# Convolution taps of the VectorE moved between attention blocks in a one-core hybrid decoder step

## The chip, the cores and the metric

The program runs on one core of a Trainium2 chip (eight cores in two dies). The metric is device time in microseconds of one execution. Engines are called by their names in the profile: PE is TensorE, DVE VectorE, ACT ScalarE, POOL GpSimd, SP SyncE.

## The reference, cut to what matters

One layer of a decoder for a prompt of 1024 tokens and 8 sample sequences of 4 tokens (1056 columns in all). One input projection feeds three branches: a gated linear recurrence, stick-breaking attention and a convolution module. The change touches the order of work in the last two:

```python
def _sb_block(q, k, v, bias, q_pos, k_pos):
    z = jnp.einsum('bhqd,bhkd->bhqk', q, k) * (SB_HEAD_DIM ** -0.5) + bias[None, :, None, None]
    mask = k_pos[None, :] < q_pos[:, None]
    log_rest = jnp.where(mask, jax.nn.log_sigmoid(-z), 0.0)
    tail = lax.cumsum(log_rest, axis=3, reverse=True) - log_rest
    A = jnp.where(mask, jnp.exp(jax.nn.log_sigmoid(z) + tail), 0.0)
    return jnp.einsum('bhqk,bhkd->bhqd', A, v)

c = _causal_dwconv(u_full, W['conv_w'][l], W['conv_b'][l])   # 31 taps per channel, before LayerNorm, swish, w_pc
```

The attention is causal in query blocks of 128 tokens: block q of the prompt looks at 128 (q + 1) keys, so block 0 is 128 keys wide and block 7 is 1024 wide.

## The kernel before, in words

Everything is kept transposed, 128 channels on the partitions and 1056 tokens along them. After an opening (RMSNorm, five projection units) come four groups, p = 0 to 3, of 128 channels each; the first three run in a loop, the last is written out. A group holds one pair of attention heads, 128 convolution channels and one recurrence head. After the groups come the branch projections, the output projection and the feed-forward part, which the diff leaves alone.

All five engines run their own program, and the order on each is written out by hand; they meet through semaphores, whose helper `wait` is a method of `Signal`. On DVE a chain semaphore (`Chain`) keeps dependent instructions apart.

**Projection units as filler.** The projection of the group after (and the gates) is cut into units. One unit is 128 output channels: 8 k-steps of 9 matmuls (hi and lo halves of the weights and of the activations, three column thirds of 352), recorded at L367. `fill(n)` on PE issues n such k-steps between attention steps, in the pattern `A_FILL = (2, 2, 3, 1)`, so one attention block holds exactly one unit. All units accumulate in the same PSUM banks 0 to 2. So the first k-step of a unit waits until ACT has copied the unit before out of PSUM (`stage_unit`, the ACTIVATE at L895). That copy stands at the head of the next block in ACT's order. When a unit is done, POOL splits the weights that come two units later (CAST L344, then TENSOR_TENSOR L346), and SP loads the next ones (L337) once the split is over.

**One attention block q**, two heads e = 0, 1:
- PE: scores, first 512 keys (L604); transposes of head 0's weights of block q-1 (L615); fill(2); from block 4 on the scores of the other keys (L604); fill(2); transposes of head 1 of block q-1 (L615); fill(3); product with the values of block q-1 (L626); fill(1), which ends the unit.
- ACT: stage_unit of the last unit (L895), copies of the scores with bias (L943), softplus of each head as Exp and Ln (L950, L952), copies of the transposed weights (L966), final exponential of each head (L958, `weights_of`). Head 1's `weights_of` is the last of the block, and the stage_unit of the next block stands behind it.
- DVE: for each head `scores_read`, the mask on the diagonal (L1272) and the clip (L1275); then for each head `tail_sum`, that is a max (L1282), a reversed scan (L1284) and a subtract (L1285), which releases `weights_of` on ACT.

Small sample work is mixed in: in block 1 PE makes the sample scores (L635) once SP's cache loads have landed; in block 2 DVE masks, clips and scans the sample row (L1293, L1294, L1301, L1303, L1304); in block 3 ACT makes its exponential (L988), for which the PE waits before it transposes it (L643); in block 4 come the sample values (L653).

**The convolution on DVE.** One tap is a multiply-add over 1024 prompt columns (L1256) and a small one over the 32 sample columns (L1257); the first tap is L1259 and L1260. Each tap first waits for the tap before it. `tap()` issues the next one and does nothing once all 31 are out. Before the change it stands at four places in each block: between mask and clip of head 0 and of head 1 (in `scores_read`), before the tail sum of head 0, and between the two tail sums. That gives taps 0 to 27 in blocks 0 to 6 and the last three in block 7, the last before the tail sum of head 0. The last tap releases SP's stores of the convolution (L432 to L435), which in SP's order stand behind a gate store that waits for ACT's copy at the head of the step after block 7.

```python
                    dg = z[:, q * P:n]
                    ch.mark(dve.tensor_tensor(dg, dg, neg, ALU.add))
                    tap()
                    ch.wait()
                    dve.tensor_scalar(l, z, ZMAX, None, ALU.min).then_inc(e_ready.sem, 1)
```

Of the kernel before, what the change touches and what calls it, by code (L numbers as in the profile page):

```python
# [40 lines left out]
QB = TP // P  # L41
Z_CHUNKS = [q if q < 4 else 4 + 2 * (q - 4) for q in range(QB + 1)]
A_FILL = (2, 2, 3, 1)
H_FILL = (4, 4, 3, 3, 3, 3, 3, 3, 3, 3, 4, 4)
GPG = 5
NGATE = 3 * KD
# [55 lines left out]
def build(nc, dr):  # L102
    ctx = ExitStack()
    with ctx:
# [84 lines left out]
        def par(name, j=0, n=1):  # L189
            a = PK[name][0] + j  # L190
            return pk[:, a:a + n]
# [367 lines left out]
        def _(pe):  # L559
# [48 lines left out]
            def turn_a(p, i):  # L608
                a_ready.wait(pe, p, i + 1)
                if i:  # L610
                    at_ready.wait(pe, p, i)
                if i == 8:
                    os_read.wait(pe, p, 1)
                for kb in range(i // 2 + 1):
                    mm = pe.transpose(banks(5, 1024)[:, kb * P:(kb + 1) * P],  # L615
                                      zb[2 * (i // 2 % 2) + i % 2][:, kb * P:(kb + 1) * P], ident)
                mm.then_inc(t_done.sem, 1)

            def values(p, q):

                at_ready.wait(pe, p, 2 * q + 2)
                if q:
                    o_read.wait(pe, p, q)
                for kb in range(q + 1):
                    for e in range(2):
                        mm = pe.matmul(ps[DH * e:DH * e + DH, 7, (q % 4) * P:(q % 4 + 1) * P],  # L626
                                       vtok[:, kb, DH * e:DH * e + DH], atv[e][:, kb * P:(kb + 1) * P],
                                       start=(kb == 0), stop=(kb == q))
                mm.then_inc(av_done.sem, 1)
# [17 lines left out]
            def sample_values(p):  # L647
                ats_ready.wait(pe, p, 1)
                pe.matmul(ps[:, 6, 256:320], vtok[0:SM, 8, :], ats[0:SM, 2, :], start=True, stop=False,
                          skip_group_check=True)  # L650
                for b in range(NSEQ):
                    for g in range(NPG):
                        mm = pe.matmul(ps[:, 6, 256 + 8 * b:264 + 8 * b], vsv[:, b, g, :], ats[:, g, 8 * b:8 * b + 8],  # L653
                                       start=False, stop=(b == NSEQ - 1 and g == NPG - 1), skip_group_check=True)
                mm.then_inc(os_done.sem, 1)
# [7 lines left out]
            def turn9(src, b0):  # L663

                for c in range(CH):
                    pe.transpose(banks(b0, 1024)[:, c * P:(c + 1) * P], src[:, c * P:(c + 1) * P], ident)
                return pe.transpose(ps[0:SM, 7, 0:P], src[:, TP:T], ident)

            def level_product(p, idx, left, right, b0, sample):
                for c in range(CH):  # L670
                    mm = pe.matmul(banks(b0, 1024)[:, c * P:(c + 1) * P], left[:, c * P:(c + 1) * P],  # L671
                                   right[:, c * P:(c + 1) * P], start=True, stop=True)
                if sample:
                    mm = pe.matmul(ps[0:SM, 7, 0:SM], left[:, TP:T], right[:, TP:T], start=True, stop=True)
                mm.then_inc(lev_done.sem, 1)

            def group(p, more):
                at_k = [0]

                def fill(n):  # L680

                    for _ in range(n):
                        jj, k = divmod(at_k[0], KD)
                        if jj < units(more):
                            unit_part(PRE + jj, p, (k,))
                            at_k[0] += 1
# [3 lines left out]
                for q in range(QB + 1):  # L690
# [4 lines left out]
                    if q:  # L695
                        turn_a(p, 2 * q - 2)
                    fill(A_FILL[0])
                    if 4 <= q < QB:
# [5 lines left out]
                    if q == 4:  # L704
                        sample_values(p)
                    fill(A_FILL[1])
                    if q:
                        turn_a(p, 2 * q - 1)
                    fill(A_FILL[2])
                    if q:  # L710
                        values(p, q - 1)
                    fill(A_FILL[3])

# [3 lines left out]
                turn9(iT, 5).then_inc(ia_turned.sem, 1)  # L717
                fill(H_FILL[0])
                qk_ready.wait(pe, p, 1)
                va_staged.wait(pe, p, 1)  # L720
                level_product(p, 0, kk, qA, 3, True)
                fill(H_FILL[1])
                for j in range(NL):
# [4 lines left out]
                    if j < 5:  # L728
                        fill(H_FILL[2 + j])
                fill(H_FILL[7])  # L730
                kd_ready.wait(pe, p, 1)
                att_read.wait(pe, p, NL + 1)
                turn9(kd, 3).then_inc(kd_turned.sem, 1)
                fill(H_FILL[8])
                kdt_staged.wait(pe, p, 1)
# [8 lines left out]
                mm.then_inc(um_done.sem, 1)  # L744
                fill(H_FILL[9])
                s_ready.wait(pe, p, 1)
# [445 lines left out]
        def _(dve):  # L1192
# [23 lines left out]
            def group(p, more):  # L1216
# [32 lines left out]
                def tap(last=False):  # L1249
                    w = taps[0]  # L1250
                    if w >= CW:
                        return
                    taps[0] += 1
                    if w:
                        ch.wait()
                        ch.mark(dve.scalar_tensor_tensor(ca, up[:, w:w + TP], cwp[:, w:w + 1], ca, ALU.mult, ALU.add))  # L1256
                        ins = dve.scalar_tensor_tensor(cs, us[:, :, w:w + TS], cwp[:, w:w + 1], cs, ALU.mult, ALU.add)  # L1257
                    else:
                        ch.mark(dve.tensor_scalar(ca, up[:, 0:TP], cwp[:, 0:1], cwp[:, CW:CW + 1], ALU.mult, ALU.add))  # L1259
                        ins = dve.tensor_scalar(cs, us[:, :, 0:TS], cwp[:, 0:1], cwp[:, CW:CW + 1], ALU.mult, ALU.add)  # L1260
                    if w == CW - 1:
                        ins.then_inc(conv_done.sem, 1)
                    else:
                        ch.mark(ins)

                def scores_read(q, e):

                    i, n = 2 * q + e, P * (q + 1)
                    z, l = zb[2 * (q % 2) + e][:, 0:n], lb[e][:, 0:n]
                    z_read.wait(dve, p, 2 * Z_CHUNKS[q + 1] - 1 + e)  # L1270
                    dg = z[:, q * P:n]
                    ch.mark(dve.tensor_tensor(dg, dg, neg, ALU.add))  # L1272
                    tap()
                    ch.wait()
                    dve.tensor_scalar(l, z, ZMAX, None, ALU.min).then_inc(e_ready.sem, 1)  # L1275

                def tail_sum(q, e):

                    i, n = 2 * q + e, P * (q + 1)
                    z, l = zb[2 * (q % 2) + e][:, 0:n], lb[e][:, 0:n]  # L1280
                    ln_ready.wait(dve, p, i + 1)
                    ch.link(dve.tensor_tensor(l, z, l, ALU.max))  # L1282
                    r = l[:, ::-1]
                    ch.link(dve.tensor_tensor_scan(r, r, r, 0.0, ALU.add, ALU.max))  # L1284
                    dve.tensor_tensor(z, z, l, ALU.subtract).then_inc(arg_ready.sem, 1)  # L1285

                zs, ls = A(A_ZS, SBK, slice(0, 64)), A(A_LS, SBK, slice(0, 64))
                for q in range(QB):
                    scores_read(q, 0)
                    scores_read(q, 1)  # L1290
                    if q == 2:
                        zs_read.wait(dve, p, 1)
                        ch.link(dve.tensor_tensor(zs[:, PAST:], zs[:, PAST:], par("neg_new", 0, SM)[0:64, :], ALU.add))  # L1293
                        dve.tensor_scalar(ls, zs, ZMAX, None, ALU.min).then_inc(es_ready.sem, 1)  # L1294
                    tap()
                    tail_sum(q, 0)
                    tap()
                    tail_sum(q, 1)
                    if q == 2:
                        lns_ready.wait(dve, p, 1)  # L1300
                        ch.link(dve.tensor_tensor(ls, zs, ls, ALU.max))  # L1301
                        r = ls[:, ::-1]
                        ch.link(dve.tensor_tensor_scan(r, r, r, 0.0, ALU.add, ALU.max))  # L1303
                        dve.tensor_tensor(zs, zs, ls, ALU.subtract).then_inc(args_ready.sem, 1)  # L1304
                while taps[0] < CW:
                    tap()

# [105 lines left out]
            with dve.Fori(0, NH - 1) as p:  # L1413
                group(p, True)
            group(NH - 1, False)


# [231 lines left out]
```

## Time and profile before

| | |
|---|---|
| median of 3 runs | 2382.62 us (2382.07 to 2383.61) |
| the profiled execution's own time | 2382.67 us |
| its span, first to last instruction | 2380.9 us |
| mean granted TensorE clock | 0.941 |
| PE busy | 2086.1 us (88%) |
| DVE busy | 1101.2 us (46%) |
| ACT busy | 610.0 us (26%) |
| POOL busy | 591.3 us (25%) |

Busy times are sums over an engine's instructions. PE is busy for 88% of the span, but that is an average: the groups fill about the first half, and there PE has gaps. In a view of stretches each row is from A to B of the span (here from the end of one stage_unit copy to the next), its length, the busy us of PE, PEld, DVE, ACT and POOL with their counts, the granted TensorE clock (PEclk), the DMA share and GB/s. An idle time in brackets behind a row says how long the engine had waited just before that instruction, and what ended the wait.

### The profile page before, as it was taken

Reading aid. Unit: us, or ns where it says so; the run is one execution under the profiler, and the core shown is the slowest. Engines: PE = TensorE matmul, PEld = TensorE weight load, DVE = VectorE, ACT = ScalarE, POOL = GpSimd, SP = SyncE. Lnnn points to the kernel's source line nnn. Section 1 sums busy time; section 2 is a strip of 40 time slices with the busy share of each in tenths; the row PEclk is TensorE's granted clock in tenths of the full one; section 3 lists DMA queues with packets and bytes.
Section 4 is the critical chain, followed back from the end, with each engine's and each line's share of the span. In section 5 each row is a group of like instructions: output and inputs, shape, how many; then the busy total and the mean of one; then the engine's idle time right before and its main releaser. Section 6 shows DMA issues by size and latency. Waiting matters only on the chain.

```text
span 2380.9 us, 32200 instructions
## 1 busy us (share of the span) xinstructions
PE 2086.1 (88%) x12832; PEld 1984.5 (83%) x12832; DVE 1101.2 (46%) x1169; ACT 610.0 (26%) x792; POOL 591.3 (25%) x392
## 2 busy tenths in 40 slices
PE   7898789977999779997787989879999999999994
PEld 5887688867888678886787889759999999999993
DVE  3267465664547655566543653362223222222235
ACT  3234322344134342334312522130101001001011
POOL 1211211121111112111212232242333332323332
PEclk9999899988999889998898999889999999999997
DMA  4221203111031111310225331311111111111121
GB/s 138 61 82 31 66 19 117 49 36 57 19 120 46 36 57 37 119 36 27 75 83 184 109 122 47 123 69 41 40 57 31 48 52 32 53 40 40 57 104 77
DMA packets 203987, 156.89 MB, mean 66 GB/s; under 512 B 15730, under 2 KB 188402, under 8 KB 203890
## 3 DMA queue, kind: packets, MB, share of 16 engines
q1 hardware_dynamic: 201698, 146.89, 19.7%
q10 hardware_dynamic: 2192, 8.65, 0.9%
q8 instruction: 68, 1.11, 0.2%
q14 instruction: 29, 0.24, 0.0%
HBM read 120.16 MB, written 35.35 MB: 65 GB/s over the span
## 4 chain that ended last, share of the span: by engine, by line
PE 68%; DVE 18%; ACT 6%; issue 5%; DMA 1%; SPq 1%; POOL 0%; POOLq 0%; DVEq 0%; ACTq 0%
PE psum L367 59%; DVE arena L1284 3%; PE psum L671 2%; DVE arena L1256 2%; DVE arena L1282 1%; DVE arena L1257 1%; PE psum L604 1%; PE psum L572 1%; DVE hid L1523 1%; DVE arena L1272 1%; PE psum L653 1%; DVE ug L1285 1%; DVE mix L1508 1%; PE psum L626 1%; DVE arena L1285 1%
## 5 line engine op out<-in xcount | busy, mean ns | idle before, releaser
L367 PE MATMUL psum<-h_hi,w_hi 128*128 128x352 f32 x2400 | 557.2, 342 | 157.3 <-ACT gate_logits L895 61.2
L367 PEld LDWEIGHTS psum<-h_hi,w_hi 128*128 128x128 f32 x2400 | 416.8, 197 | 184.6 <-issue 163.4
L367 PE MATMUL psum<-h_lo,w_hi 128*128 128x352 f32 x2400 | 533.9, 332 | 0.0
L367 PE MATMUL psum<-h_hi,w_lo 128*128 128x352 f32 x2400 | 530.7, 330 | 0.0
L367 PEld LDWEIGHTS psum<-h_lo,w_hi 128*128 128x128 f32 x2400 | 425.5, 196 | 0.0
L367 PEld LDWEIGHTS psum<-h_hi,w_lo 128*128 128x128 f32 x2400 | 424.4, 194 | 0.0
L344 POOL CAST w_hi<-w_raw 128x1024 fp32r<-128x1024 f32 x60 | 71.8, 1197 | 967.5 <-PE psum L367 948.6
L357 POOL CAST w_hi<-w_raw 128x512 fp32r<-128x512 f32 (+1 forms) x128 | 96.5, 754 | 736.6 <-PE psum L367 642.0
L359 POOL TENSOR_TENSOR w_lo<-w_raw,w_hi 128x512 fp32r<-128x512 f32 (+1 forms) x128 | 227.8, 1780 | 10.3
L1173 ACT ACTIVATE hid<-psum 128x1056 f32<-128x1056 f32 x32 | 33.7, 1054 | 583.1 <-PE psum L367 583.1
L367 PE MATMUL psum<-hid_hi,w_hi 128*128 128x352 f32 x768 | 166.4, 325 | 10.8 <-DVE hid_lo L1525 10.8
L1532 DVE TENSOR_TENSOR ff_sum<-ff_sum,psum 128x1056 f32<-128x1056 f32 x56 | 70.2, 1254 | 227.4 <-PE psum L367 227.4
L1523 DVE TENSOR_TENSOR hid<-hid 128x1056 f32<-128x1056 f32 x32 | 54.4, 1699 | 254.2 <-ACT hid L1173 254.2
L367 PE MATMUL psum<-hid_lo,w_hi 128*128 128x352 f32 x768 | 166.7, 325 | 0.0
L367 PE MATMUL psum<-hid_hi,w_lo 128*128 128x352 f32 x768 | 165.7, 324 | 0.0
L346 POOL TENSOR_TENSOR w_lo<-w_raw,w_hi 128x1024 fp32r<-128x1024 f32 x60 | 156.9, 2614 | 4.8
L1256 DVE SCALAR_TENSOR_TENSOR arena<-arena,conv_w_now 128x1024 f32<-128x1024 f32 x120 | 153.7, 1281 | 2.1
L367 PEld LDWEIGHTS psum<-hid_hi,w_hi 128*128 128x128 f32 x768 | 130.9, 188 | 13.0 <-DVE hid_lo L1525 13.0
L367 PEld LDWEIGHTS psum<-hid_lo,w_hi 128*128 128x128 f32 x768 | 131.1, 188 | 0.0
L367 PEld LDWEIGHTS psum<-hid_hi,w_lo 128*128 128x128 f32 x768 | 130.6, 188 | 0.0
L1284 DVE TENSOR_TENSOR_SCAN arena<-arena 128x128 f32<-128x128 f32 (+7 forms) x64 | 109.5, 1711 | 2.2
L1272 DVE TENSOR_TENSOR arena<-arena,params 128x128 f32<-128x128 f32 x48 | 22.1, 461 | 163.3 <-ACT arena L943 163.3
(237 smaller groups left out, 2417.9 us busy)
## 6 DMA issues: line engine op xcount, KB each, us to landing
w_raw<-in_w_in SPq DMA_DIRECT2D x60, 512.0 KB, 4.1
w_raw<-in_w_ff SPq DMA_DIRECT2D x32, 512.0 KB, 4.0
w_raw<-in_w_ff SPq DMA_DIRECT2D x64, 256.0 KB, 2.7
g_d<-gate_logits SPq DMA_DIRECT2D x24, 528.0 KB, 3.1
gates<-g_d SPq DMA_DIRECT2D x24, 528.0 KB, 3.6
arena<-in_xT SPq DMA_DIRECT2D x8, 528.0 KB, 7.3
x_again<-in_xT SPq DMA_DIRECT2D x1, 4224.0 KB, 13.8
x_d<-x_again ACTq DMA_DIRECT2D x8, 528.0 KB, 2.7
```

Source lines behind the costliest of these rows:

```text
L344: pool.tensor_copy(wh[:, s, :, :], raw[:, s, :, :]).then_inc(w_hi_set, 1)
L346: pool.tensor_tensor(wl[:, s, :, :], raw[:, s, :, :], wh[:, s, :, :].bitcast(F32), ALU.subtract).then_inc(w_split, 1)
L357: pool.tensor_copy(wh[:, slot, 0:kt, :], raw[:, slot, 0:kt, :]).then_inc(w_hi_set, 1)
L359: pool.tensor_tensor(wl[:, slot, 0:kt, :], raw[:, slot, 0:kt, :], wh[:, slot, 0:kt, :].bitcast(F32), ALU.subtract).then_inc(w_split, 1)
L367: mm = pe.matmul(ps[:, b0 + g, 0:GW], w[:, slot, k, :], x[:, k, g * GW:(g + 1) * GW], start=(k == 0 and w is wh and x is xh), stop=(k == k ...
L671: mm = pe.matmul(banks(b0, 1024)[:, c * P:(c + 1) * P], left[:, c * P:(c + 1) * P], right[:, c * P:(c + 1) * P], start=True, stop=True)
L1256: ch.mark(dve.scalar_tensor_tensor(ca, up[:, w:w + TP], cwp[:, w:w + 1], ca, ALU.mult, ALU.add))
L1272: ch.mark(dve.tensor_tensor(dg, dg, neg, ALU.add))
L1284: ch.link(dve.tensor_tensor_scan(r, r, r, 0.0, ALU.add, ALU.max))
L1285: dve.tensor_tensor(z, z, l, ALU.subtract).then_inc(arg_ready.sem, 1)
L1523: dve.tensor_tensor(h, h, h, ALU.mult).then_inc(hid_sq, 1)
L1532: dve.tensor_tensor(v3(acc[:, j, :]), v3(acc[:, j, :]), psg(3 * (j % 2)), ALU.add)\
```

## The change

A new tuple `EARLY` says how many extra taps stand at the end of each block. In blocks 0 to 3 all four old places stay, and 4, 4, 2 and 1 taps are added behind the tail sum of head 1 (in block 2 behind the sample's scan too). In blocks 4 to 7 only the place before the tail sum of head 0 keeps its tap. So blocks 0 to 3 hold 8, 8, 6 and 5 taps and blocks 4 to 7 one each, 31 in all as before, and the last stands where it stood.

```diff
+EARLY = (4, 4, 2, 1, 0, 0, 0, 0)
...
                     dg = z[:, q * P:n]
                     ch.mark(dve.tensor_tensor(dg, dg, neg, ALU.add))
-                    tap()
+                    if q < 4:
+                        tap()
                     ch.wait()
...
                     tap()
                     tail_sum(q, 0)
-                    tap()
+                    if q < 4:
+                        tap()
                     tail_sum(q, 1)
...
                         dve.tensor_tensor(zs, zs, ls, ALU.subtract).then_inc(args_ready.sem, 1)
+                    for _ in range(EARLY[q]):
+                        tap()
                 while taps[0] < CW:
                     tap()
```

## Rows read from the trace of the kernel before

**Rows 1.** Who waited for whom, PE: total us, times, longest us

```profile
PE psum L367 <- ACT gate_logits L895: 61.2, 11, 7.3
PE psum L367 <- ACT gA L895: 32.8, 4, 8.3
...
PE psum L643 <- ACT arena L988: 10.3, 4, 3.0
```

**Rows 2.** Group 1, blocks 2, 4 to 7: length, busy PE, PEld, DVE, ACT, POOL, PEclk

```profile
425.05:441.15 16.10, 14.52 (x95) 13.16 (x93) 15.28 (x21) 6.53 (x16) 5.39 (x4) 1.00 0.20 67
...
460.47:483.04 22.57, 22.57 (x143) 21.09 (x144) 13.29 (x18) 8.68 (x16) 3.44 (x3) 0.85 0.14 48
483.04:507.10 24.06, 16.95 (x120) 15.15 (x120) 17.20 (x18) 9.45 (x15) 6.81 (x4) 0.96 0.08 22
507.10:534.65 27.55, 19.38 (x125) 17.76 (x125) 18.40 (x18) 10.32 (x15) 4.74 (x2) 0.81 0.20 58
534.65:562.23 27.58, 18.88 (x123) 17.37 (x123) 18.11 (x16) 11.38 (x15) 6.29 (x2) 0.81 0.00 1
```

**Rows 3.** DVE in order of time, group 1, block 6 and end of block 7

```profile
514.37 1.28 DVE L1256 SCALAR_TENSOR_TENSOR arena<-arena,conv_w_now 128x1024 f32<-128x1024 f32 x1
...
515.86 0.63 DVE L1275 TENSOR_SCALAR arena<-arena 128x896 f32<-128x896 f32 x1
...
521.22 2.02 DVE L1284 TENSOR_TENSOR_SCAN arena<-arena 128x896 f32<-128x896 f32 x1
...
524.29 1.28 DVE L1256 SCALAR_TENSOR_TENSOR arena<-arena,conv_w_now 128x1024 f32<-128x1024 f32 x1
525.49 1.03 DVE L1257 SCALAR_TENSOR_TENSOR arena<-arena,conv_w_now 128x32 f32<-128x32 f32 x1
...
527.55 4.04 DVE L1284 TENSOR_TENSOR_SCAN arena<-arena 128x896 f32<-128x896 f32 x1
531.63 1.09 DVE L1285 TENSOR_TENSOR arena<-arena 128x896 f32<-128x896 f32 x1
...
549.24 2.29 DVE L1284 TENSOR_TENSOR_SCAN arena<-arena 128x1024 f32<-128x1024 f32 x1
...
553.97 3.01 DVE L1284 TENSOR_TENSOR_SCAN arena<-arena 128x1024 f32<-128x1024 f32 x1
557.01 3.18 DVE L1285 TENSOR_TENSOR ug<-ug,arena 128x1024 f32<-128x1024 f32 x1
```

**Rows 4.** POOL in order of time, groups 0 (block 1) and 1 (blocks 0, 6)

```profile
136.88 1.04 POOL L344 CAST w_hi<-w_raw 128x1024 fp32r<-128x1024 f32 x1 [20.17 <-PE psum L367]
...
403.10 2.37 POOL L346 TENSOR_TENSOR w_lo<-w_raw,w_hi 128x1024 fp32r<-128x1024 f32 x1
...
524.89 1.58 POOL L344 CAST w_hi<-w_raw 128x1024 fp32r<-128x1024 f32 x1 [22.22 <-PE psum L367]
526.55 3.16 POOL L346 TENSOR_TENSOR w_lo<-w_raw,w_hi 128x1024 fp32r<-128x1024 f32 x1
```

**Rows 5.** PE in order of time, three matmuls a row, start of block 6

```profile
507.23 1.22 PE L367 MATMUL psum<-h_hi,w_hi 128*128 128x352 f32 x3 [7.25 <-ACT gate_logits L895]
508.25 1.08 PE L367 MATMUL psum<-h_lo,w_hi 128*128 128x352 f32 x3
...
513.91 0.64 PE L367 MATMUL psum<-h_lo,w_hi 128*128 128x352 f32 x3
```

**Rows 6.** DVE in order of time, group 0, blocks 1 and 2

```profile
118.53 0.29 DVE L1272 TENSOR_TENSOR arena<-arena,params 128x128 f32<-128x128 f32 x1 [1.68 <-ACT arena L943]
...
131.47 0.43 DVE L1282 TENSOR_TENSOR arena<-ug,arena 128x256 f32<-128x256 f32 x1 [4.58 <-ACT arena L952]
...
138.31 2.24 DVE L1272 TENSOR_TENSOR arena<-arena,params 128x128 f32<-128x128 f32 x1 [5.22 <-ACT arena L943]
...
152.33 2.60 DVE L1301 TENSOR_TENSOR arena<-arena 64x288 f32<-64x288 f32 x1
```

**Rows 7.** One line of the program: min/median/max ns of all 120

```profile
L1256 DVE SCALAR_TENSOR_TENSOR arena<-arena,conv_w_now x120: 1269/1282/1287, 107.8 to 1126.8; 128x1024 f32<-128x1024 f32 x120
```

## The prediction

> **What bounds it.** The list of PE's waits comes first: the longest, 61.2 us in 11 waits, is PE's filler waiting for ACT's copy of a gate unit, and 32.8 us in 4 more for the copy of gA [rows 1]. That copy is ACT's first work in a block, but in ACT's order it stands behind the last exponential of the block before, which DVE's last subtract releases. So PE waits for DVE's chain. The view of stretches says where: blocks 6 and 7 last 27.55 and 27.58 us with PE busy for 19.38 and 18.88, block 5 24.06 with 16.95, while block 4 is 22.57 us long and PE is busy for all of it [rows 2]. DVE is busy for 17 to 18 us in blocks 5 to 7, in one unbroken run from the mask to the last subtract. There every DVE microsecond is one on the path; in block 4 none is. The wait repeats once a block, four groups long. Block 2 is another kind: DVE is busy 15.28 of its 16.10 us [rows 2], and at its end hangs the sample chain (DVE, ACT's exponential, PE's transpose), for which PE waits up to 3.0 us in each of four groups [rows 1].
>
> **What leaves the wide blocks.** Eleven taps of a group move: three each from blocks 4, 5 and 6, two from block 7. No DMA moves with them, and the last tap keeps its place, so SP's and POOL's orders stay.
>
> A tap between mask and clip costs the time from its start to the clip's, 515.86 - 514.37 = 1.49 us [rows 3]. The one between the tail sums runs from 524.29 to 526.5, 2.1 us, because its small half takes 1.03 us [rows 3] while a split cast is on POOL [rows 4].
>
> Taking these out also moves the last tail sum off POOL's next instruction. In block 6 the scan of head 1 takes 4.04 us against 2.02 for head 0 [rows 3]; POOL's split ran from 526.55 for 3.16 us, the scan began at 527.55 [rows 4]. POOL starts when PE ends its unit, which stays about where it is against the block's start, while the DVE chain then ends some 5 us earlier. So the 2.0 us go too.
>
> - Block 4: 0. PE has no gap.
> - Block 5: 2 x 1.49 + 2.1 + 2.0 = 7.1 us; 24.06 becomes 16.9, just the 16.95 that PE needs [rows 2].
> - Block 6: the same 7.1, and the clock. Before block 6 PE idles 7.25 us and then works at the lower level of its clock, 1.08 us for three matmuls; later it is 0.64, so the upper one [rows 5]. Over the five slow rows that is about 2.3 us. With the gap gone (under 1 us left) I take it back whole: 9.5 us. 27.55 becomes 18.0; PE needs 19.38 - 2.3 = 17.1.
> - Block 7: two taps 3.0; the scan's 3.01 against 2.29 and the subtract's 3.18 against the 1.09 of block 6 [rows 3] give 2.8 more, of which I leave 1.1 in, since this chain is the longest and its end still meets a cast (1.04 us where nothing is in its way [rows 4]); the clock 2.3. Together 6.9 us; 27.58 becomes 20.7.
> - The step behind block 7: PE still idles about 4 us instead of 7.3, 0.8 us of slow clock back.
>
> Sum per group: 24.4 us. ACT does not take over: Exp and Ln of head 0 end about when the one tap left does.
>
> The Trainium skill ("SBUF — State Buffer", Who interferes with whom) states that a VectorE instruction with two SBUF inputs and a GpSimd instruction that reads SBUF shut each other out for a whole instruction. The rows with a stretched scan agree; the sum would be the same without the page.
>
> **What the narrow blocks pay.** A tap behind another costs 1.49 us too.
>
> Block 0 gets four, 5.95 us. In group 0 DVE idles 1.68 us before block 1 [rows 6], so block 1 begins 4.3 us late. It has a wait of 4.58 us before its last tail sum [rows 6], for ACT and PE, not for DVE: absorbed. The same wait in the other three groups is 4.2 to 5.3 us. In group 1 a split begins (403.10) just as the new taps would start [rows 4], which adds its 2.4 us, of which about 1.1 overflow.
>
> Block 1 gets four, 5.95 us from 133.1 (the wait's end at 131.47 and 1.6 us of tail sum), into an idle of 5.22 us before block 2 [rows 6]. But a cast of 1.04 us, from 136.9 on, and its split of 2.4 us [rows 4] fall there; before, the first mask of block 2 waited out part of it (2.24 us long against 0.29). Taps, cast and split in a row end at 133.1 + 5.95 + 3.4 = 142.5, mask and clip work resumes then instead of at 140.6: 2.1 us late.
>
> Block 2 is DVE-bound, so the 2.1 stay. Before, 2.8 us of its end were lost to the next split (L1301 over 288 columns took 2.60 us where a max over 256 took 0.43 [rows 6]; the subtract before it lost the other 0.6); with DVE busy all through it loses 3.4. Late by 2.8. Two more taps, 3.0: 5.8 us late. The sample chain passes this on to PE one to one, as PE waits there already [rows 1]. A longer idle before it costs perhaps 0.5 us of slow clock: 6.3 us.
>
> Block 3: one tap in front of block 4, where DVE waits for PE: 0.
>
> Bounds for this part: no collision with POOL at all leaves only the two taps, 3.0 us. Nothing absorbed at all is 11 x 1.49 + 3 x 3.4 + 0.5 = 27.1 us. I take 6.3, since each idle it uses has its row.
>
> **Sum.** 4 x 24.4 = 97.6 us out, 4 x 6.3 + 1.1 = 26.3 us in: 71.3 us less. Against the profiled execution's 2382.67 us (span 2380.9), which is the median within 0.1 us, that makes 2311 us, 3% faster. About 0.2%, 5 us, is what a measurement can tell here from no change.
>
> **Rivals.**
> 1. *The taps do not meet POOL.* For it: no big tap half was ever stretched, 1269 to 1287 ns in all 120 [rows 7]. Against it: the small half, the same operation, was [rows 3], and no big half ever began while a split ran. The narrow part is then 3.0 us: 2382.7 - 4 x 21.4 = 2297 us. Chance 0.15.
> 2. *The wide blocks keep their slow start.* PE's gaps shrink, but the clock falls again with them, or the scans meet POOL still, because PE's unit ends earlier as well. For it: block 4 has no idle and yet a granted clock of 0.85 [rows 2]. Either costs 4 to 5 us a group: 2311 + 4 x 4.6 = 2330; both together some 2345 us. Chance 0.2. The Trainium skill ("TensorE: Matmul & The Clock Gate", The HAM clock gate) has the clock fall after an idle time, and gaps under 1 us would keep it up.
> 3. *Slower.* The sample chain in block 3 carries all of it: if none of the DVE idle in blocks 0 and 1 can be used, because PE waits for those blocks' results too, the narrow part is 27.1 us against 24.4. That gives 2382.7 + 4 x 2.7 = 2394 us. It decides from 24.4 us of lateness a group; the 4.58 and 5.22 us of idle [rows 6] speak against it. Chance 0.02.
> 4. *No effect.* PE would have to be the bound of blocks 5 to 7, with the waits moved only. PE's 7 to 10 us of gaps there [rows 2] speak against it: 2383 us. Chance 0.03.
>
> **How the numbers follow.** My forecast, 2311 and a few us around it, has 0.6; faster by over 0.2% are it and rivals 1 and 2, 0.95. The range reaches to rival 1 below, 2294, and past the first half of rival 2 above, 2334; outside lie both mishaps of rival 2 at once, 3 and 4.
>
> **What will show it.** Right: PE's 15 waits for the copy of a gate unit or gA shrink from 7 to 8 us to under 1 before blocks 6 and 7, and to about 4 behind block 7; the stretches of blocks 5, 6 and 7 last 17, 18 and 21 us; scans of 768 and 896 columns are as long for head 1 as for head 0; the first filler rows of block 6 take 0.64 us; block 4 stays at 22.6. The transpose behind ACT's L988 comes 6 us later in the group, and a small tap half or a mask in block 1 is stretched to over 2 us. Wrong: scans of 4 us still, 1.08 us filler rows at the head of blocks 6 and 7, or narrow blocks late by under 4 or over 9 us.

## The result and the profile after

The changed kernel takes 2305.28 us in the median (2304.59 to 2307.91, 4 runs) against 2382.35 us for the kernel before, run beside it: a ratio of 0.9678 (0.9661 to 0.9694), 77 us less. The forecast was 2311 us, range 2294 to 2334. The profiled execution's span is 2302.8 us, 78.1 us shorter, and the mean granted clock rose from 0.941 to 0.954.

PE's waits, to be read against [rows 1]: total us, times, longest us. The first two lines are the longest; the third is the wait for the sample's exponential, the last the one for gA.

```profile
PE psum L368 <- ACT qA L896: 21.7, 4, 5.4
PE psum L368 <- ACT gate_logits L896: 18.7, 7, 4.0
...
PE psum L644 <- ACT arena L989: 6.3, 4, 2.3
PE psum L368 <- ACT gA L896: 4.4, 4, 1.1
```

(The program's lines moved down by one to five: L895 is L896 now, the scan L1284 is L1286, and so on.) The waits for a gate unit's copy fell from 61.2 to 18.7 us and for gA from 32.8 to 4.4. The wait for the sample's exponential fell too, from 10.3 to 6.3. At the top now stands one that was short before: 21.7 us for the copy of qA at the head of block 3, where the kernel before waited 6.9 us in all.

The stretches of group 1, blocks 2 and 4 to 7, in the order and with the columns of [rows 2]:

```profile
409.45:429.24 19.79, 14.51 (x95) 13.15 (x93) 19.37 (x26) 6.52 (x16) 6.42 (x4) 0.95 0.23 73
447.83:470.40 22.57, 22.57 (x143) 21.14 (x144) 9.03 (x12) 8.67 (x17) 3.43 (x3) 0.85 0.14 48
470.40:487.33 16.93, 16.93 (x120) 15.16 (x120) 10.14 (x12) 9.58 (x16) 4.10 (x4) 1.00 0.11 32
487.33:505.61 18.28, 17.17 (x126) 15.54 (x125) 11.34 (x12) 10.55 (x16) 4.48 (x3) 1.00 0.18 59
505.61:526.19 20.58, 16.62 (x123) 15.39 (x123) 13.23 (x12) 11.54 (x16) 5.86 (x3) 1.00 0.09 26
```

Block 5 is now as long as PE is busy in it (16.93 us), blocks 6 and 7 have 1.1 and 4 us of gap, and in all three the clock is at its upper level throughout (1.00). Block 2 went the other way: 16.10 to 19.79 us, with DVE busy for 19.37. Block 4 did not move.

DVE in block 6 of group 1, which answers to [rows 3]:

```profile
492.14 0.29 DVE L1273 TENSOR_TENSOR arena<-arena,params 128x128 f32<-128x128 f32 x1 [6.62 <-ACT arena L944]
492.47 0.63 DVE L1277 TENSOR_SCALAR arena<-arena 128x896 f32<-128x896 f32 x1
...
493.87 1.28 DVE L1257 SCALAR_TENSOR_TENSOR arena<-arena,conv_w_now 128x1024 f32<-128x1024 f32 x1
...
496.35 2.02 DVE L1286 TENSOR_TENSOR_SCAN arena<-arena 128x896 f32<-128x896 f32 x1
...
500.54 2.02 DVE L1286 TENSOR_TENSOR_SCAN arena<-arena 128x896 f32<-128x896 f32 x1
502.59 1.09 DVE L1287 TENSOR_TENSOR arena<-arena 128x896 f32<-128x896 f32 x1
```

The chain from the first mask to the last subtract's end is 11.5 us (492.14 to 503.68) instead of 18.7. The clip follows the mask after 0.33 us, and both scans take 2.02 us; the stretched one of 4.04 us is gone. POOL's next instructions show why:

```profile
502.89 1.69 POOL L345 CAST w_hi<-w_raw 128x1024 fp32r<-128x1024 f32 x1 [13.72 <-PE psum L368]
504.66 2.37 POOL L347 TENSOR_TENSOR w_lo<-w_raw,w_hi 128x1024 fp32r<-128x1024 f32 x1
```

The cast comes 15.6 us after the block's start, only 2.2 us earlier than before (PE's clock), while DVE's chain ends 16.4 us after it, 9 us earlier than before. So the split begins a microsecond after the chain is over. Here it is the cast that waits for the subtract (1.69 us against 1.04).

The end of block 1 in group 0 shows where the moved taps pay (it answers to [rows 6]):

```profile
131.71 0.42 DVE L1284 TENSOR_TENSOR arena<-ug,arena 128x256 f32<-128x256 f32 x1 [0.87 <-ACT arena L953]
...
137.40 1.03 DVE L1258 SCALAR_TENSOR_TENSOR arena<-arena,conv_w_now 128x32 f32<-128x32 f32 x1
138.46 3.48 DVE L1257 SCALAR_TENSOR_TENSOR arena<-arena,conv_w_now 128x1024 f32<-128x1024 f32 x1
141.87 0.24 DVE L1258 SCALAR_TENSOR_TENSOR arena<-arena,conv_w_now 128x32 f32<-128x32 f32 x1
142.03 0.28 DVE L1273 TENSOR_TENSOR arena<-arena,params 128x128 f32<-128x128 f32 x1
```

Of the 4.58 us that DVE waited before the last tail sum of block 1, 0.87 are left: the four taps at the end of block 0 went into it. The four at the end of block 1 fill the 5.22 us of idle and meet POOL's cast (the small half of 1.03 us) and its split. A big tap half of 3.48 us is something that no tap of the kernel before showed. The first tap of block 2 starts at 142.34 where it was 140.58, 1.8 us late.

Taken over the four groups, from the end of one copy at the head of a block to the next (the same measure as the stretches above):

| us | block 1 | block 2 | block 3 | block 4 | block 5 | block 6 | block 7 | step behind |
|---|---|---|---|---|---|---|---|---|
| before | 19.3-20.6 | 16.1 | 17.9-19.5 | 21.0-22.6 | 24.05 | 26.9-27.6 | 27.2-27.6 | 17.8-18.1 |
| after | 19.0-21.9 | 19.8 | 18.6-21.5 | 21.0-22.6 | 16.93 | 18.24-18.28 | 20.57-20.59 | 17.4-17.6 |

Blocks 5 to 7 and the step behind them sum to 387.2 us before and 293.3 after, 93.9 less; blocks 1 to 4 to 309.2 and 323.7, 14.5 more. Block 0 in front of them sums to 69.1 and 68.3.

### The profile page after: what moved, and what is told of

Same layout as the page of the kernel before. It is cut to its first block, busy times and chain, and to the rows that moved or that the text cites. A ratio compares the mean times of both kernels' runs of the same rounds, so it can differ in the third digit from the quotient of the medians.

```text
span 2302.8 us, 32197 instructions
## 1 busy us (share of the span) xinstructions
PE 2075.3 (90%) x12832; PEld 1973.8 (86%) x12832; DVE 1074.8 (47%) x1169; ACT 612.0 (27%) x792; POOL 578.7 (25%) x392
## 3 DMA queue, kind: packets, MB, share of 16 engines
q1 hardware_dynamic: 201698, 146.89, 20.3%
## 4 chain that ended last, share of the span: by engine, by line
PE 70%; DVE 16%; ACT 6%; issue 5%; DMA 1%; SPq 1%; POOL 0%; POOLq 0%; DVEq 0%; ACTq 0%
PE psum L368 60%; PE psum L672 3%; DVE arena L1286 3%; DVE arena L1257 2%; DVE arena L1284 1%; PE psum L605 1%; PE psum L627 1%; DVE arena L1258 1%; PE psum L573 1%; PE psum L616 1%; DVE hid L1528 1%; DVE mix L1513 1%; PE psum L654 1%; DVE arena L1287 1%; PE psum L636 1%
## 5 line engine op out<-in xcount | busy, mean ns | idle before, releaser
L368 PE MATMUL psum<-h_hi,w_hi 128*128 128x352 f32 x2400 | 550.5, 338 | 100.4 <-ACT qA L896 21.7
L368 PEld LDWEIGHTS psum<-h_hi,w_hi 128*128 128x128 f32 x2400 | 411.3, 194 | 127.6 <-issue 107.1
L368 PEld LDWEIGHTS psum<-h_lo,w_hi 128*128 128x128 f32 x2400 | 420.5, 194 | 0.0
L1257 DVE SCALAR_TENSOR_TENSOR arena<-arena,conv_w_now 128x1024 f32<-128x1024 f32 x120 | 164.6, 1371 | 2.0
L347 POOL TENSOR_TENSOR w_lo<-w_raw,w_hi 128x1024 fp32r<-128x1024 f32 x60 | 147.2, 2454 | 4.8
L1286 DVE TENSOR_TENSOR_SCAN arena<-arena 128x128 f32<-128x128 f32 (+7 forms) x64 | 97.3, 1521 | 2.2
L368 PE MATMUL psum<-o_hi,w_hi 128*128 128x352 f32 x288 | 66.6, 341 | 23.6 <-DVE o_lo L1468 11.7
```

The lines of the kernel that those rows point to most:

```text
L347: pool.tensor_tensor(wl[:, s, :, :], raw[:, s, :, :], wh[:, s, :, :].bitcast(F32), ALU.subtract).then_inc(w_split, 1)
L368: mm = pe.matmul(ps[:, b0 + g, 0:GW], w[:, slot, k, :], x[:, k, g * GW:(g + 1) * GW], start=(k == 0 and w is wh and x is xh), stop=(k == k ...
```

## The experiments

The theory is the prediction's: the DVE chain is the path of blocks 5 to 7 and not of block 4, its taps, a collision with POOL and a slow clock all hang on it, and the narrow blocks pay through the sample chain.

**Where the moved taps go: `e1_late`.** The extra taps are left out of blocks 0 to 3, so the loop behind block 7 issues them.

```diff
-EARLY = (4, 4, 2, 1, 0, 0, 0, 0)
+EARLY = (0, 0, 0, 0, 0, 0, 0, 0)
```

> Blocks 0 to 3 hold four taps each as before the change, blocks 4 to 7 one, and the 11 others stand behind block 7, where VectorE had 23 us of idle. Theory (the narrow blocks' lateness is a real cost, and the wide blocks gain whatever becomes of the taps): blocks 1 to 4 as before the change, blocks 5 to 7 at 16.9, 18.3 and 20.6 us as after it; the 14.4 us that the four groups' narrow blocks lost come back, 2305 - 14 = 2291 us (by the prediction's own 26.3 us it would be 2285). Rival (the 11 taps, 16.4 us, delay SyncE's stores and loads behind block 7 or meet the splits there): the step behind block 7 or the recurrence part is longer by up to 16 us a group, 2291 to 2355 us.

Measured: 2290.46 us, 0.9614 (0.9598 to 0.963). As the theory had it. Blocks 2 and 3 are back at 16.1 and 17.9 to 20.6 us, and blocks 5 to 7 keep 16.9, 18.3 and 20.6. So the two parts add up, and the narrow part of the change costs about 15 us. DVE behind block 7:

```profile
248.75 3.36 DVE L1257 SCALAR_TENSOR_TENSOR arena<-arena,conv_w_now 128x1024 f32<-128x1024 f32 x1
...
271.82 1.26 DVE L1321 SCALAR_TENSOR_TENSOR arena<-fT,arena 128x1056 f32<-128x1056 f32 x1 [4.71 <-ACT arena L1032]
```

Eleven taps, the first stretched by a split, and still 4.71 us of idle before the recurrence part needs DVE.

**Is DVE's busy time the bound, or the chain? `e2_early_only`.** The extra taps stay, and no place is closed: block 4 has four taps, blocks 5 to 7 none.

```diff
-                    if q < 4:
-                        tap()
+                    tap()
...
-                    if q < 4:
-                        tap()
+                    tap()
```

> The extra taps of blocks 0 to 3 stay and no place in the wide blocks is taken away, so that block 4 issues four taps and blocks 5 to 7 none. Theory (the one tap left before head 0's tail sum lies in the shadow of ScalarE's Exp and Ln, and block 4 is bound by TensorE): no block changes by more than 0.3 us, 2305 within 3 us. Rival (VectorE's own work is the bound of blocks 5 to 7, so each tap less is worth 1.49 us): 3 x 1.49 x 4 = 18 us less, 2287 us.

Measured: 2301.16 us, 0.9659 (0.9642 to 0.9676), 4 us less than the changed kernel where the theory had it within 3; the intervals of the two overlap. The rival's 18 us for the three taps a group less in blocks 5 to 7 are excluded. Block 5 is 16.66 us instead of 16.93, block 6 18.15, block 7 as it was. In place of the tap stands a wait for ACT:

```profile
205.19 0.56 DVE L1276 TENSOR_SCALAR arena<-ug 128x768 f32<-128x768 f32 x1
206.75 0.96 DVE L1283 TENSOR_TENSOR arena<-arena 128x768 f32<-128x768 f32 x1 [0.99 <-ACT arena L953]
```

One tap a block costs at most 0.3 us there, and block 4 takes its three at no cost (21.0 to 22.6 us, as ever).

**How the narrow blocks pay: `e4_narrow_only` and `e3_sample_free`.** The first has the extra taps in blocks 0 to 3 and all the old places too; taps beyond the 31st are issued again from the first on, so its convolution holds 11 summands too many. The lines that add `EARLY` and its loop and those that move the convolution's last tap to the 42nd are left out here:

```diff
-                    w = taps[0]
-                    if w >= CW:
+                    w = taps[0] % CW
+                    if taps[0] >= CW + 11:
                         return
```

> The narrow blocks as after the change, the wide ones with all their taps as before it: 11 taps are issued a second time there, so the convolution output holds 11 summands too many. Theory: blocks 5 to 8 as before the change; the narrow part alone costs what the traces show, 14 us, 2382.5 + 14 = 2397 us. By the prediction's term 26.3 us, 2409 us; by its rival 1 (taps do not meet GpSimd's splits) 12 us, 2394 us.

Measured: 2397.0 us against 2382.2, 1.0055 (1.0033 to 1.0077): 15 us (8 to 18) slower. The narrow part alone is a loss. The interval leaves out the 26 us that the prediction charged; it does not tell the 12 us of rival 1 from the 14 of the traces. The stretched taps do: this kernel's trace has them as the changed kernel's has, with a big half of 3.50 us at 137.41.

The second moves the two taps from the end of block 2 to the end of block 3.

```diff
-EARLY = (4, 4, 2, 1, 0, 0, 0, 0)
+EARLY = (4, 4, 0, 3, 0, 0, 0, 0)
```

> The extra taps are 4, 4, 0, 3: the two at the end of block 2 now stand at the end of block 3. Theory (TensorE waits for the sample chain before its transpose, by 1.6 us a group on average after the change, and after that it is its own bound): blocks 3 get shorter by about that wait, 4 to 7 us in all, 2299 to 2301 us; block 4 is not longer, as VectorE idles 6.5 us before it. Rival of the prediction (one to one): 2 x 1.49 us in each group, 12 us less, 2293 us.

Measured: 2293.75 us, 0.9623 (0.9603 to 0.9642), 12 us under the changed kernel. The theory's 4 to 7 us were too few, and the rival's 12 came out, but not one to one: the transpose comes 25.5 us after block 2's start in all four groups, where the changed kernel has 26.7, so only 1.2 of the 3.0 us of taps arrive there. PE's wait before it disappears from the list (6.3 us in the changed kernel), as the theory had it. Block 3 falls from 18.6-21.5 us to 17.2-17.5, which is 7.8 us in the four groups. Of these, 4.1 are in group 0, the only group in which the changed kernel's PE worked at the lower level of its clock behind this wait (of 2.27 us there, and 1.2 to 1.5 in the others). The slow stretch behind the wait for qA stays. PE at the head of block 3, group 1 of this run:

```profile
424.40 1.22 PE L368 MATMUL psum<-h_hi,w_hi 128*128 128x352 f32 x3 [5.42 <-ACT qA L896]
425.41 1.08 PE L368 MATMUL psum<-h_lo,w_hi 128*128 128x352 f32 x3
```

Another 3.2 us are in block 4, 21.0 us in all four groups here and 22.6 in two of them in the changed kernel (granted clock 0.92 and 0.85). No run shows whether the moved taps do that.

**The wide blocks in halves: `e5_between_late` and `e6_clips_late`.** In both, `EARLY` is all zeros. The first closes only the place between the tail sums from block 4 on, the second only those between mask and clip.

That is the changed kernel with the condition taken off again at the other place, for e5 in `scores_read`, for e6 between the tail sums:

```diff
-EARLY = (4, 4, 2, 1, 0, 0, 0, 0)
+EARLY = (0, 0, 0, 0, 0, 0, 0, 0)
...
-                    if q < 4:
-                        tap()
+                    tap()
```

> Against the kernel before, blocks 4 to 6 lose only the tap between the two tail sums; these and the places freed in block 7 are made up behind block 7. The taps between mask and clip stay. Theory (VectorE and GpSimd shut each other out for whole instructions, and what counts is where the chain's end falls against GpSimd's work): in block 5 the cast would begin 15.2 us after the block's start, the scan at 15.4 waits for it, the split runs from 18.0 to 20.4 and the last subtract waits for that, so the block lasts some 23 us, where the tap alone would give 21.9; blocks 6 and 7 also keep most of their length, 25 to 27 us. Total 2382 less 4 x (1 to 4), 2366 to 2378 us. Rival (the prediction's terms added up, tap 2.1 and scan 2.0 each): blocks 5 and 6 at 19.9 and 23.4 us, 2382 - 4 x 8.2 = 2349 us.

Measured: 2373.92 us, 0.9955 (0.9939 to 0.9971), 10 us less, where the terms of the prediction added up would have given 33. Block 5 is 22.67 us, not 19.9. Its last tail sum, and POOL beside it:

```profile
208.65 2.56 DVE L1285 TENSOR_TENSOR_SCAN arena<-arena 128x768 f32<-128x768 f32 x1
211.25 2.91 DVE L1286 TENSOR_TENSOR ug<-ug,arena 128x768 f32<-128x768 f32 x1
```

```profile
208.57 1.04 POOL L345 CAST w_hi<-w_raw 128x1024 fp32r<-128x1024 f32 x1 [12.67 <-PE psum L368]
209.69 3.67 POOL L347 TENSOR_TENSOR w_lo<-w_raw,w_hi 128x1024 fp32r<-128x1024 f32 x1
```

The scan (1.76 us by itself) waits for the cast, the split waits for the scan, and the subtract (0.96 us by itself) waits until the split ends at 213.36. Taking out 2.1 us of work only moved the collision from the scan to the scan and the subtract behind it. The block got 1.4 us shorter. Block 6 lasts 26.0 to 26.5 us, as the theory had it; block 7 gained nothing at 27.0 to 28.2 us, where the theory had 25 to 27.

> Against the kernel before, blocks 4 to 7 lose only the taps between mask and clip; those are made up behind block 7. The tap between the tail sums stays. Theory (as for the run with the other half): block 5 ends its tail sums 16.6 us after its start, with a cast of 1 us in between, so it lasts 19.5 us; block 6 keeps some of its slow clock, 20 to 24 us, block 7 22 to 24 us; in all 4 x (4.5 + 5 + 4) = 54 us less, 2328 us, within 12 us. Rival (terms added up, two taps of 1.49 us a block and no collision gone): 4 x 3 x 3.0 = 36 us less, 2346 us.

Measured: 2320.03 us, 0.9734 (0.9717 to 0.9751), 64 us less. That is more than either figure, and inside the theory's band of 12 us: block 5 at 18.93 us, block 6 at 20.3 to 21.8, block 7 at 21.9 to 23.3. Two halves of 10 and 64 us make 92 in `e1_late`. That fits a gain that comes in only when the chain's end clears POOL's split and no slow stretch follows PE's gap: the granted clock of block 7 is 0.80 to 0.82 in e5, 0.87 to 0.94 here and 0.98 to 1.00 in `e1_late`. No run tells the share of the one from that of the other.

**Versions meant to beat both: `e7_block2_free`, `e9_both_sample_first`, and `e10_after_sample_first`.** The first takes all taps out of block 2, which DVE bounds, gives block 4 its four, block 0 one more, and leaves 11 for the end.

```diff
-EARLY = (4, 4, 2, 1, 0, 0, 0, 0)
+EARLY = (1, 0, 0, 0, 0, 0, 0, 0)
...
-                    if q < 4:
+                    if q < 5 and q != 2:
                         tap()
...
-                    tap()
+                    if q != 2:
+                        tap()
                     tail_sum(q, 0)
-                    if q < 4:
+                    if q < 5 and q != 2:
                         tap()
```

> A version meant to beat both: block 2 has no taps, blocks 1, 3 and 4 four each, block 0 five, blocks 5 to 7 one each, and the 11 others stand behind block 7. Theory (block 2 is bound by VectorE and the sample chain by its end): block 2 falls from 16.1 us to TensorE's 14.5, the waits of up to 3 us for the sample's exponential (11.8 us in all in the run with the 11 taps behind block 7) and for the qA copy (6.9 us) go: 2290 - 19 = 2271 us, 2265 to 2280 with the clock. Rival (those waits give way to another, such as ScalarE's or the cache loads): no better than the run with the 11 taps behind block 7, 2290 us.

Measured: 2281.77 us, 0.9568 (0.9552 to 0.9584). It is 9 us faster than `e1_late`, not 19, and just outside the expected 2265 to 2280. Block 2 falls to 14.07 us, as expected, and the qA wait is gone from the list. But the wait for the sample's exponential stays (12.5 us in all). ACT's rows in block 3 say why:

```profile
153.09 0.49 ACT L967 ACTIVATE arena<-psum 128x384 f32<-128x384 f32 x1
156.63 0.63 ACT L951 ACTIVATE arena<-arena 128x512 f32<-128x512 f32 x1 [3.05 <-DVE arena L1277]
157.29 0.63 ACT L953 ACTIVATE arena<-arena 128x512 f32<-128x512 f32 x1
157.83 0.43 ACT L989 ACTIVATE arena<-arena 64x288 f32<-64x288 f32 x1
```

The exponential (L989) starts at 157.83. Its argument has been ready since 149.5 us, but in ACT's order it stands behind the softplus of block 3, which waits for DVE's clip of that block. The wait had two causes, one behind the other. So the next two kernels move it:

```diff
+                    if q == 3:
+                        args_ready.wait(act, p, 1)
+                        z = A(A_ZS, SBK, slice(0, 64))
+                        act.activation(z, z, ACT.Exp).then_inc(as_ready.sem, 1)
                     if q < QB:
                         softplus(q, 0)
...
-                    if q == 3:
-                        args_ready.wait(act, p, 1)
-                        z = A(A_ZS, SBK, slice(0, 64))
-                        act.activation(z, z, ACT.Exp).then_inc(as_ready.sem, 1)
```

> The changed kernel with that one edit on ScalarE alone. Theory (the part of the narrow blocks' cost that reaches TensorE is this wait, 6.3 us in all, and the slow clock behind it): 2305.5 - 6 to 14 = 2292 to 2300 us; block 2 stays at 19.8 us, block 3 gets shorter by 1.5 us or more. Rival (the cost is the qA copy at the head of block 3, 21.7 us of waiting, alone): no change, 2305 us.

Measured: 2295.53 us, 0.9638 (0.9612 to 0.9663), 10 us under the changed kernel. The intervals just touch, but the slowest of these four executions (2300.14 us) is faster than each of the eight of the changed kernel (2302.76 and more). It is as the theory had it: the wait is gone, block 2 stays at 19.8, block 3 is at 16.8 to 17.5 us. The 21.7 us of waiting for qA are all still there, so these 10 us did not come from them. They are not free for that: the next kernel, with the same order on ACT, has neither the taps in block 2 nor that wait, and is another 22 us faster.

> The version with block 2 free of taps, and ScalarE's exponential of the sample moved in block 3 ahead of head 0's softplus instead of behind it. Theory (in that version TensorE's wait of 3.1 us for the exponential stood behind the softplus of block 3, which waits for VectorE's first clip there, and no longer behind block 2): the 12.5 us of that wait go, and some of the slow clock behind it, 2282 - 12 - 0 to 8 = 2262 to 2270 us. Rival (the wait moves to the transposes behind it): no change, 2282 us.

Measured: 2273.23 us, 0.9547 (0.9519 to 0.9575), the fastest here. In the profiles block 3 falls from 19.7-20.8 to 16.3 us in all four groups, 17 us together, but the medians differ by 8.5 us only, less than the 12 to 20 expected. The two intervals overlap, though no execution of `e7_block2_free` (2279.66 us and more) is as fast as the slowest of this kernel (2279.24). Part of the difference is that the profiled execution of `e7_block2_free` took 2286.7 us, 5 us above its median, and that of this kernel 2270.6, 3 us below. Block 4 gives back 2.6 us: it lasts 22.5 us in two groups here. What else takes the gain back is open; of the four executions, the two near 2270 us have a mean granted clock of 0.962 and 0.959, the two near 2277 have 0.955. PE at the sample's transpose, `e7_block2_free` first and this kernel behind it:

```profile
158.40 0.45 PE L644 MATMUL psum<-params,arena 64*128 64x64 f32 x2 [3.12 <-ACT arena L989]
...
158.88 1.25 PE L368 MATMUL psum<-h_hi,w_hi 128*128 128x352 f32 x3
159.93 1.08 PE L368 MATMUL psum<-h_lo,w_hi 128*128 128x352 f32 x3
```

```profile
153.95 0.34 PE L644 MATMUL psum<-params,arena 64*128 64x64 f32 x2
...
154.27 0.75 PE L368 MATMUL psum<-h_hi,w_hi 128*128 128x352 f32 x3
154.86 0.64 PE L368 MATMUL psum<-h_lo,w_hi 128*128 128x352 f32 x3
```

The 3.12 us of wait bring nearly 6 us of matmuls at the lower level of the clock after them (1.08 us for three against 0.64). By an estimate from these rows, 5.9 x (1 - 0.64 / 1.08), such a wait costs about 2.4 us on top.

**The same kernel again: `e8_after_again`.** The changed kernel with no edit.

> The changed kernel once more beside the other runs of this chip: 2305 us, 0.968 of the kernel before, within 4 us. If the lengths of blocks 1, 3 and 4 are set by where the clock's falls come, they differ here from the first profile in steps of about 1.5 us while blocks 2, 5, 6 and 7 are the same within 0.1 us; if they are fixed by the program, all are the same.

Measured: 2305.96 us, 0.9668 (0.9652 to 0.9684). Blocks 2, 5, 6 and 7 repeat within 0.1 us (19.8, 16.92-16.93, 18.24-18.28, 20.57-20.59). In the others the same groups differ: block 3 of group 0 is 20.1 us here and 21.5 in the first profile (granted clock 0.83 and 0.77), block 4 of group 0 22.6 and 21.0 (0.85 and 0.92), of group 3 21.0 both times. So these steps go with the clock. The largest difference is in block 1 of group 2, 23.6 us here and 19.0 there, of which block 0 in front of it takes back 2.2. There PE waits for the sample's cache loads as well (L636: 6.6 us in two waits here, 2.9 us in one there).

## Why the prediction was right

Its mechanism held in the wide blocks. In the narrow ones it named the right collisions and the right chain, but had their price wrong. The terms came out thus (us a group, forecast and measured):

- Block 4: 0, and 0 but for steps of 1.6 in single groups, either way.
- Block 5: 7.1 and 7.1. The scan's collision and the taps are as costed, and PE became the bound at 16.93 us, as [rows 2] said it would.
- Block 6: 9.5 and 9.1 (27.34 in the mean to 18.26). The slow clock went whole: 1.00 in the stretch, where [rows 2] had 0.81.
- Block 7: 6.9 and 6.9. Of the 1.1 us that were left in for the cast, 0.65 show in the last subtract (1.87 us for 1.22 in group 0). The subtract before the change had been set against the 1.09 us of a narrower one; a subtract of this width takes 1.22.
- The step behind: 0.8 and 0.4, in the second profile 0.1.
- The narrow blocks: 26.3 in all and 14.5. With block 0 they cost 13.6 in the first profile and 14.9 in the second, 3.4 and 3.7 us a group. **This is the term that was mis-sized.** The prediction had named narrow blocks late by under 4 us as a sign that it is wrong, and that sign came: its account of them does not stand as it was given.

The wide part brought 93.9 us where 97.6 were forecast, the narrow part cost 12 us less than forecast. So the 6 us between 2311 and 2305 are a larger miss partly made up by a smaller one, and the closeness is in part luck.

Three steps of that term were too high. First, "late by 2.8" at the end of block 2: the second split costs DVE the same with its row full as it did before (the small half's 0.8 and 2.0 us in a scan, together the 2.8 of before), so the lateness stayed at the 1.8 us with which the block began. (The 2.1 us forecast for that start stand beside 142.5 and 140.6, which are 1.9 apart.) Second, group 1: its first new tap is held up by the split just as foreseen,

```profile
386.21 3.45 DVE L1257 SCALAR_TENSOR_TENSOR arena<-arena,conv_w_now 128x1024 f32<-128x1024 f32 x1
...
403.13 0.42 DVE L1284 TENSOR_TENSOR arena<-ug,arena 128x256 f32<-128x256 f32 x1 [0.59 <-ACT arena L953]
```

but 0.59 us of idle is still left at the end of block 1, so nothing overflowed. Third, "PE waits there already, one to one": measured from block 2's start, the transpose came 4.4 us later in every group (26.7 us for 22.35), near the 1.8 + 3.0 of DVE's lateness and not 6. And PE paid most of it elsewhere, in a place for which the prediction has no term. In group 0 it began its filler at 157.97 instead of 154.04, behind the qA copy, which head 1's tail sum of block 2 held up: that had started 2.6 us late (the 1.8 and the stretched small half) and had the split in its scan (2.98 us for 0.96). The rows of the two kernels, before and after:

```profile
154.04 0.72 PE L367 MATMUL psum<-h_hi,w_hi 128*128 128x352 f32 x3 [1.72 <-ACT qA L895]
```

```profile
157.97 1.22 PE L368 MATMUL psum<-h_hi,w_hi 128*128 128x352 f32 x3 [5.41 <-ACT qA L896]
```

The wait before the transpose fell from 2.96 to 2.27 us. In groups 1 to 3 block 3 lasts 18.6 us, where it lasted 17.9 to 19.5. So blocks 2 and 3 together are 2.9 to 4.5 us longer in these groups and 5.8 in group 0, on average 4.

Of the signs, PE's waits before blocks 6 and 7 (at most 1.1 us) and behind block 7 (4.0), the lengths of blocks 5 to 7, the equal scans and the fast filler rows came. A stretched small tap half or mask in block 1 did not: it was a big half, at 3.48 us.

Rival 1 fell by that tap, though its 12 us for the narrow part are nearer to the 14.5 than the forecast's 26.3, and its 2297 us are 8 from the measured time where 2311 is 6. Rival 2 fell by the clock of 1.00 and by the scans of 2.02 us. Its collisions are real all the same: `e5_between_late` met them when the chain was cut by too little. Rival 3 fell by the idle that was used (4.58 us down to 0.87 in block 1), and `e4_narrow_only` puts the narrow part alone at 15 us in all four groups, where this rival has 27 in each. Rival 4 had nothing.

The Trainium skill ("SBUF — State Buffer", Who interferes with whom) says that whichever starts first of a VectorE instruction with two SBUF inputs and a GpSimd instruction that reads SBUF holds the other off for a whole instruction. The traces agree in both directions: a big tap half held up for 2.2 us by a split, and a cast held up for 0.65 us by a subtract.

## What to carry to other kernels

Look at where a stretch is bound before moving work into it or out: 11 taps taken from the DVE-bound blocks 5 to 7 and from block 4 brought 94 us, and the same 11 put into blocks that were bound by DVE in one place cost 15, while behind block 7 they cost nothing that shows (blocks 5 to 7 and the step behind sum to 294.6 us there, and to 293.3 and 294.5 in the two profiles of the changed kernel). What a chain gains by losing an instruction depends on what its end then meets: 2 us out brought 1.4 in block 5 and everything out 7.1. A wait that remains after its cause is gone (the sample's exponential) has a second cause in the waiting engine's own order; moving that one instruction took 10 us off the median by itself.

## What the runs showed that was not expected

A gap of 3 us on PE can cost more than 3 us: in `e7_block2_free` the lower clock that followed it for nearly 6 us (1.08 against 0.64 us for three matmuls) cost about 2.4 us more. Not every gap of that length does so: in `e1_late` PE waits 2.96 us before this transpose in each group, and the granted clock of block 3 is 1.00 in group 1 and 0.91 in group 0. This is part of why removing 6.3 us of waiting brought 10 to 12; much of the rest lies in block 4, whose clock steps from one execution to the next, and the runs do not say why. The same kernel, profiled twice, has blocks 3 and 4 of one group differ by 1.4 and 1.6 us and block 1 of another by 4.6, while blocks 2, 5, 6 and 7 repeat within 0.1 us; a change in a block with such a stretch is better read from the waits than from the block's length in one profile.
